# Down-projection weights in 16 KB runs, and a hidden activation turned in four shifted blocks

## The reference, cut to what matters

```
for e in range(32):
    y = (silu(t @ w_gate[e]) * (t @ w_up[e])) @ w_down[e]     # 1024 -> 512 -> 1024
    out = out + combine[:, e:e+1] * y
```

## Time and profile before

| | |
|---|---|
| median of three runs | 893.41 us (892.76 to 894.4) |
| time of the profiled execution | 893.44 us |
| its span, first to last instruction | 891.8 us |
| mean granted TensorE clock over the span | 0.980 |
| busy: PE, PEld, DVE, ACT, POOL | 92%, 64%, 37%, 23%, 17% |
| DMA packets in all | 71744, 265.18 MB |

### The profile page before, as it was taken

The page is one execution under the profiler, slowest core; times in us unless marked ns, Lnnn a source line. Parts: engine busy times, 40 slices in busy tenths (PEclk is TensorE's granted clock), DMA queues, the critical chain, the costliest instruction groups (busy, mean ns, idle before and its releaser), DMA issues.

```text
span 891.8 us, 15452 instructions
## 1 busy us (share of the span) xinstructions
PE 821.4 (92%) x5317; PEld 569.0 (64%) x5318; DVE 330.2 (37%) x616; ACT 200.7 (23%) x296; POOL 155.8 (17%) x241
## 2 busy tenths in 40 slices
PE   7999999999999999999899999989989999997860
PEld 6888887888888888886455554455545555544430
DVE  3799997841645246258111011110111101110107
ACT  4633435142643324141000000000000000000003
POOL 4232901000220000010212222112202222112100
PEclk9999999999999999999999999999999999999995
DMA  8693321723234938559999999999999999999977
GB/s 256 144 181 113 103 86 19 179 80 134 72 118 162 408 122 315 225 207 347 418 421 419 417 423 420 425 423 424 424 421 423 424 423 425 422 424 422 423 324 276
DMA packets 71744, 265.18 MB, mean 297 GB/s; under 512 B 29526, under 2 KB 30550, under 8 KB 54516
## 3 DMA queue, kind: packets, MB, share of 16 engines
q1 hardware_dynamic: 65428, 254.10, 74.8%
q0 software_dynamic: 6128, 10.45, 3.1%
q10 hardware_dynamic: 144, 0.02, 0.0%
HBM read 256.59 MB, written 16.52 MB: 306 GB/s over the span
## 4 chain that ended last, share of the span: by engine, by line
PE 78%; SPq 6%; DMA 6%; DVE 5%; issue 2%; ACT 2%; POOL 0%; DVEq 0%; POOLq 0%; ACTq 0%
PE ps L1095 36%; PE ps L465 22%; PE ps L481 11%; DMA slot_x<-in_exp_w_gate 5%; SPq L448 4%; PE ps L1080 2%; SPq L446 2%; PE ps L471 1%; DVE pair L716 1%; DVE pair L721 1%; PE ps L1072 1%; DVE hl L773 1%; PE ps L603 1%; DMA ssm<-choice_rows 1%; SPq L493 0%
## 5 line engine op out<-in xcount | busy, mean ns | idle before, releaser
L716 DVE TENSOR_TENSOR pair<-pair,ps 128x256 f32<-128x256 f32 x32 | 13.5, 421 | 334.9 <-PE ps L465 334.9
L1095 PE MATMUL ps<-h_hi,w_hi 128*128 128x512 f32 x280 | 109.2, 390 | 0.0
L1095 PE MATMUL ps<-h_hi,w_lo 128*128 128x512 f32 x280 | 109.0, 389 | 0.0
L1095 PE MATMUL ps<-h_lo,w_hi 128*128 128x512 f32 x280 | 108.9, 389 | 0.0
L1530 DVE TENSOR_TENSOR w_lo<-raw,w_hi 128x1024 fp32r<-128x1024 f32 x56 | 72.5, 1296 | 95.6 <-ACT w_hi L1334 94.9
L1334 ACT CAST w_hi<-raw 128x1024 fp32r<-128x1024 f32 x59 | 62.1, 1056 | 188.2 <-PE ps L1095 188.2
L465 PE MATMUL ps<-ssm,pair 128*64 128x256 f32 x832 | 95.2, 384 | 5.8 <-DMA ssm<-in_exp_w_gate 4.2
L465 PEld LDWEIGHTS ps<-ssm,pair 128*64 128x64 f32 x832 | 63.0, 139 | 42.5 <-issue 17.2
L787 ACT COPY late<-ps 128x512 f32<-128x512 f32 x35 | 20.5, 587 | 296.3 <-PE ps L481 296.3
L877 POOL DMA_INDIRECT choice_rows<-late,put_now x35 | 35.6, 1018 | 289.3 <-ACT late L787 239.9
L1095 PEld LDWEIGHTS ps<-h_hi,w_lo 128*128 128x128 f32 x280 | 52.6, 188 | 11.0
(11 more groups left out here) (342 smaller groups left out, 1225.4 us busy)
## 6 DMA issues: line engine op xcount, KB each, us to landing
ssm<-in_exp_w_gate SPq DMA_DIRECT2D x16, 2048.0 KB, 21.5
raw<-in_w_in SPq DMA_DIRECT2D x40, 512.0 KB, 3.9
au<-in_exp_w_up SPq DMA_DIRECT2D x8, 2048.0 KB, 24.8
ssm<-in_exp_w_up SPq DMA_DIRECT2D x8, 2048.0 KB, 21.0
ssm<-in_exp_w_down SPq DMA_DIRECT2D x8, 2048.0 KB, 21.4
hl<-in_exp_w_down SPq DMA_DIRECT2D x8, 2048.0 KB, 25.0
slot_x<-in_exp_w_gate SPq DMA_DIRECT2D x8, 2048.0 KB, 29.3
raw<-in_exp_w_down SPq DMA_DIRECT2D x8, 2048.0 KB, 28.0
```

Source lines behind the costliest of these rows:

```text
L716: nc.vector.tensor_tensor(act_cols, silu_cols, up_now, ALU.mult).then_inc(act_ready, 1)
L1095: t = nc.tensor.matmul(bank, lhs, rhs, start=k == 0 and n == 0, stop=k == 2 * count - 1 and n == 2)
```

## The change

Down weights are read as index (p, j): partition p holds the hidden rows 4p to 4p+3 in one run of 16 KB. So hidden half h now belongs to partitions 64h to 64h+63 of the down weights. In set 3 the two halves stay: j 0 and 1, then j 2 and 3, 8 KB each on a partition.

The product is written as 4 blocks of 64 columns (a step of four words on both operands), and a second instruction repeats the first block as a fifth. TensorE turns four blocks of 128 columns, each shifted by 64, so that block j holds hidden columns j of the lower half on partitions 0 to 63, and columns j+1 on partitions 64 to 127. VectorE copies the lower partitions of it (64 x 256), ScalarE the upper ones of the other half in two instructions (64 x 192 and 64 x 64). TensorE waits for both. Of `turn_x`, three transposes now stand ahead of `turn_act` and one behind. The down product has as many matmuls as before, of the same shapes.

```diff
-        silu, act_ = pair[:, 1024:1280], pair[:, 1280:1536]
-        actT = pair[:, 1536:1792].rearrange("p (j n) -> p j n", j=2)
+        silu, act_ = pair[:, 1024:1280], pair[:, 1536:1536 + (KF + 1) * CAP]
+        actT = pair[:, 1280:1536].rearrange("p (j n) -> p j n", j=KF)
...
-                 "down": exp_w_down[0].rearrange("e (h p j) n -> e p h (j n)", p=P, j=2)}
+                 "down": exp_w_down[0].rearrange("e (p j) n -> e p (j n)", p=P)}
...
-        at_bank = ps[:, B_AT, 0:256].rearrange("p (j n) -> p j n", j=2)
-        up_now, silu_cols = (a.rearrange("p (c j) -> p j c", j=2) for a in (ps[:, B_UP, 0:F // 2], silu))
-        act_cols = act_.rearrange("p (j c) -> p j c", j=2)
+        at_bank = ps[:, B_AT].rearrange("p (j n) -> p j n", j=KF)
+        up_now, silu_cols = (a.rearrange("p (c j) -> p j c", j=KF) for a in (ps[:, B_UP, 0:F // 2], silu))
+        act_cols = act_.rearrange("p (j c) -> p j c", j=KF + 1)
...
         def turn_act():
-            for j in range(2):
-                t = nc.tensor.transpose(at_bank[:, j], act_[:, P * j:P * (j + 1)], ident[:])
+            for j in range(KF):
+                t = nc.tensor.transpose(at_bank[:, j], act_[:, CAP * j:CAP * j + P], ident[:])
             return t
+        def low_half(copy):
+            return copy(actT[0:CAP], at_bank[0:CAP, :, 0:CAP])
+        def high_half(copy):
+            copy(actT[CAP:P, 1:KF], at_bank[CAP:P, 0:KF - 1, CAP:P])
+            return copy(actT[CAP:P, 0], at_bank[CAP:P, KF - 1, CAP:P])
...
-                    t = nc.tensor.matmul(ps[CAP * c:CAP * (c + 1), bank], actT[:, j, CAP * h:CAP * (h + 1)],
-                                         w[:, 2 * h + j, W * c:W * (c + 1)], start=n == 0, stop=n == 3)
+                    t = nc.tensor.matmul(ps[CAP * c:CAP * (c + 1), bank], actT[:, j], w[:, j, W * c:W * (c + 1)],
+                                         start=j == 0, stop=j == KF - 1)
+        def activated():
+            nc.vector.tensor_tensor(act_cols[:, 0:KF], silu_cols, up_now, ALU.mult)
+            return nc.vector.tensor_tensor(act_cols[:, KF], silu_cols[:, 0], up_now[:, 0], ALU.mult)
...
-                turn_x(pe, xg[after], 0, 2)
+                turn_x(pe, xg[after], 0, 3)
                 pe.wait_ge(act_ready, e + 1)
                 turn_act().then_inc(at_full, 1)
-                turn_x(pe, xg[after], 2, 4).then_inc(xt_full, 1)
-                pe.wait_ge(actT_ready, e + 1)
+                turn_x(pe, xg[after], 3, 4).then_inc(xt_full, 1)
+                pe.wait_ge(actT_ready, e * 2 + 2)
...
-            nc.vector.tensor_tensor(act_cols, silu_cols, up_now, ALU.mult).then_inc(act_ready, 1)
+            activated().then_inc(act_ready, 1)
...
-            nc.vector.tensor_copy(actT, at_bank).then_inc(actT_ready, 1)
+            low_half(nc.vector.tensor_copy).then_inc(actT_ready, 1)
...
             def turn(e, b, nth, first):
+                if not first:
+                    gated(e, False)
+                act.wait_ge(at_full, e + 1)
+                if not first:
+                    act.wait_ge(done["down"], e)
+                high_half(nc.scalar.copy).then_inc(actT_ready, 1)
```

More of the change, by code:

```diff
@@ L373, in trunk @@
         OV_XGT, OV_PRODUCT, OV_ACTT, OV_DVE = 1, 2, 3, 3
-        OV_SILU, OV_RES, OV_ACT = 1, 2, 2
+        OV_SILU, OV_ACTT_HIGH, OV_RES, OV_ACT = 1, 2, 3, 3
         def full(eng, name):
@@ L435, in weights @@
             dst = slots[EW[w][kind]]
[L436 to L440, removed]
+            if not isinstance(e, int):
                 src = src.rearrange("e p n -> (e p) n")
             if w == SETS - 1 and kind != "gate":
-                if kind == "up":
-                    dst, src = slot_runs[EW[w][kind]], src.rearrange("p (h n) -> p h n", h=2)
+                dst, src = slot_runs[EW[w][kind]], src.rearrange("p (h n) -> p h n", h=2)
                 for h, half_in in enumerate((signal, rest_in[kind])):
@@ L519, in experts_sync @@
             weights(sp, 3, "up", 3, ew_in[3]["up"])
-            down3, down3_src = slot_runs[EW[3]["down"]], w_src["down"][3]
+            down3, down3_src = slot_runs[EW[3]["down"]], w_src["down"][3].rearrange("p (h n) -> p h n", h=2)
             def residual_half(h, half_in):
@@ L637, in experts_tensor @@
             banks_free(6, 7)
-            pe.wait_ge(actT_ready, 1)
+            pe.wait_ge(actT_ready, 2)
             pe.wait_ge(ew_in[0]["down"], 16)
@@ L678, in second_block @@
                     turn_act().then_inc(at2_full, 1)
-                    pe.wait_ge(actT2_ready, before + 1)
+                    pe.wait_ge(actT2_ready, before * 2 + 2)
                     pe.wait_ge(res2_ready, before + 1)
@@ L703, in over @@
                 pe.wait_ge(ov_dve, o_ * OV_DVE + OV_ACTT)
-                if not first:
-                    pe.wait_ge(ov_act, o_ * OV_ACT)
+                pe.wait_ge(ov_act, o_ * OV_ACT + OV_ACTT_HIGH)
                 down(0, B_RES[0]).then_inc(ov_pe, 1)
@@ L736, in second_part @@
                     v.wait_ge(second_done, before * 3 + 3 + DONE["up"])
[L737 removed]
+                    activated().then_inc(act2_ready, 1)
                     v.wait_ge(at2_full, before + 1)
[L739 removed]
+                    low_half(nc.vector.tensor_copy).then_inc(actT2_ready, 1)
             second_part(0)
@@ L756, in over @@
                     v.wait_ge(done["down"], NE)
-                nc.vector.tensor_copy(actT, at_bank).then_inc(ov_dve, 1)
+                low_half(nc.vector.tensor_copy).then_inc(ov_dve, 1)
             each_over(v, over)
@@ L804, in turn @@
                     nc.scalar.activation(silu, ps[:, B_GATE, 0:HALF], ACT.Silu).then_inc(silu2_ready, 1)
+                    act.wait_ge(at2_full, before + 1)
+                    high_half(nc.scalar.copy).then_inc(actT2_ready, 1)
                     results(res2, B_RES2, second_done, before * 3 + 3 + DONE["down"], res2_ready, second_rows, before * 16 + 16)
@@ L830, in over @@
                 nc.scalar.activation(silu, ps[:, B_GATE, 0:HALF], ACT.Silu).then_inc(ov_act, 1)
+                act.wait_ge(ov_pe, o_ * OV_PE + OV_AT)
+                if first:
+                    act.wait_ge(done["down"], NE)
+                high_half(nc.scalar.copy).then_inc(ov_act, 1)
                 if first:
```

8 lines of the change are left out of this document (3 added, 5 removed).

## The result

The changed kernel takes 905.62 us (median of four runs, 902.73 to 907.0) where the kernel before takes 893.4. The ratio is 1.0132 (95% interval 1.0118 to 1.0146): slower by 1.3%, clear of the noise, 2.0 us from the predicted 903.6 and inside the range. The profiled execution took 904.46 us for a span of 902.7.

What follows compares the result with a forecast made beforehand. The DMA stream was taken to set the end, TensorE 13.8 us ahead; 34 passes of 0.69 us add 23.5, making TensorE last, with a span of 902.0 us and 903.6 predicted, range 894.5 to 912.

Steps and rivals of the forecast that it cites:

- TensorE becomes last: Expert stage: TensorE's chain, not the DMA stream, sets the end, reaching expert 31 at 860.6 us.
- The slack of 13.8 us: At expert 31's gate product: without weight waits TensorE would start at 837.1 us instead of 850.86; added work is free up to this.
- its weights have landed some ten microseconds before: Expert 31's gate weights land at 848.8 to 850.9 us, before TensorE's chain arrives at 860.6.
- The step of four words: VectorE's products of silu and up: SBUF operand pays 0.24 us a pass over 256 + 64 columns, bounds 0 and 0.47.
- both operands pay: Rival at VectorE's products: SBUF and PSUM operands both pay for the step, d 0.92, time 911.7 us; 14 in 100.
- The second product: VectorE's 128x64 product for the repeated block: 222 ns less 0.08 overlap adds 0.14 us a pass.
- Four transposes for two: TensorE's turning of the activation: 0.72 us for four against 0.44 for two adds 0.28 us a pass.
- The copies: After the transposes: VectorE's half stays 0.42 us, ScalarE's two pieces end 0.03 later; 0.03 us a pass, bounds 0 and 0.15.
- d: What one pass from up to down gets longer: 0.14 + 0.24 + 0.28 + 0.03 = 0.69 us.
- the formula: Whole kernel, as long as TensorE is last: time = 879.5 + 35 d, crossing the old time at d = 0.40.
- the 0.2 that I took off for the down weights: Behind expert 31's gate product: the wait for the second half of the down weights, 0.49 us idle, loses 0.2.
- what could break the sum: Named risks: TensorE fetching longer loop code (single gaps of 1 to 2 us), both operands slowing the product, transposes under a hidden gap.

Runs made afterwards that it cites:

- the doses: The kernel before with one, two or four extra VectorE 128x64 products between up and down in each pass: 892.77, 893.54 and 896.69 us.
- contiguous form: The changed kernel with both operands of the silu-and-up products read contiguously, output not the reference's: 896.88 us, ratio 1.0042.
- longer runs alone: The kernel before with only the down weights loaded in 16 KB runs, output not the reference's: 891.45 us, ratio 0.9979.
- one operand: The changed kernel with ScalarE writing silu in block order, so only the PSUM operand keeps the step of four words: 897.29 us, ratio 1.0052.
- Early: The changed kernel with silu in block order and the main product announced alone; only the fourth transpose waits for the repeated block: 895.47 us, ratio 1.0025.
- pieces: The changed kernel with silu in block order and the product in three separately announced pieces, two token-row transposes on either side: 895.68 us, ratio 1.0019.
- Four products: The kernel before with four extra VectorE 128x64 products behind each silu-and-up product, ahead of the signal to TensorE: 896.69 us, ratio 1.0045.
- the two empty ones: The kernel before with a never-run branch of 28 or 4 transposes in TensorE's loop, most likely left out at build: 893.55 and 892.95 us.

## Why the prediction was right, and where it was lucky

**TensorE becomes last: shown.** The chain of after is on TensorE through the whole expert stage with no weight load, its waits for DMA there are gone, and the doses show slack first and the price behind it (0.26 x 34 costs nothing, 0.52 x 34 does). The slack of 13.8 us at the very end carried the case. Its other half, "its weights have landed some ten microseconds before", did not hold: they landed at 813.41 + 40.1 = 853.5, 6.6 us before the product and later than the 848.8 to 850.9 of the prediction, which took the DMA stream as independent of TensorE. Here that changed nothing; in two forms below it did.

**The step of four words: shown, size right.** Taken as 0.24 us a pass, it measured 0.24 (contiguous form against after). The groups by form of the kernel after, 425 to 900 us, against the earlier trace rows:

```profile
L488 DVE TENSOR_TENSOR pair<-pair,ps 128x256 f32<-128x256 f32 x34 | 20.9, 615 | 344.0 <-PE ps L460 344.0
...
L489 DVE TENSOR_TENSOR pair<-pair,ps 128x64 f32<-128x64 f32 x34 | 8.6, 253 | 0.0
```

615 against 421 ns is 0.76 ns a column, where the eight-word reduction had given 0.73. That not both operands pay was right too: with the step on the PSUM operand alone the product took 421 ns. For the SBUF operand the Trainium skill, "SBUF — State Buffer", section "Door 1: The DMA port swizzle", wants at least two hits in a line of 16 bytes for full rate. The traces agree: a step of two words is free (421 ns), one of four isn't (615 ns).

**The second product: right.** 0.14 with the step's part in the other term; one more product of 128x64 put the period at 12.22, 0.12 more.

**Four transposes for two: over-sized.** I took the row of four in a row, 0.72, minus 0.44. In the place itself they take 0.66, so 0.23 instead of 0.28: the row came from another stage.

**The copies: over-sized.** 0.48 from the copies to the down product before and after, so nothing instead of 0.03. ScalarE's pieces are 0.31 and 0.21, as worked out, and the half on VectorE sets the same 0.42. Their small errors together with the 0.02 at the product make d 0.59 and not 0.69.

**What hid that.** With the measured d the formula gives 879.5 + 35 x 0.59 = 900.2, 4.3 us below the profiled execution. The sum lacked 3.0 us ahead of expert 31 (837.1 + 34 x 0.59 = 857.2, found 860.15) and 1.3 behind it (902.7 - 860.15 = 42.55 us, where I had 40.9 - 0.2 + 0.59 = 41.3). The two errors, +3.5 us from 35 x 0.10 and -4.3, nearly cancel in this execution; against the median the formula is 5.4 short. That the forecast came within 2.0 us is luck in this part. Behind expert 31, 1.1 us is the scatter of its rows, 3.54 us in the chain of after and 2.41 in that of before, and the 0.2 that I took off for the down weights wasn't there: from the start of the last down product to the copy of its result it is 3.70 us in both kernels. Of the 3.0 us ahead of it, 2.9 can be placed. TensorE's waits of 425 to 870 us that nothing releases, in the kernel before and in the one after (sum, count, longest):

```profile
PE ps L465 <- issue: 4.4, 3, 2.1
```
```profile
PE ps L460 <- issue: 5.6, 4, 1.9
```

That is 1.2 us more, in one more wait of the kind that the prediction had named as what could break the sum: it stands in the loop's first pass, at 498.69 in the chain, and 31 instruction packets were loaded instead of 30. Another 1.7 us is the clock of one execution, just ahead of the stage. The same windows of the kernel before and of the one after (us, busy time of PE, PEld, DVE, ACT and POOL with instructions, granted clock, DMA share, GB/s):

```profile
407.00:409.00 2.00, 2.00 (x12) 0.70 (x10) 1.90 (x13) 0.00 (x0) 0.00 (x0) 1.00 1.00 297
```
```profile
405.00:407.00 2.00, 2.00 (x12) 0.97 (x11) 1.89 (x10) 0.00 (x0) 0.00 (x0) 0.72 1.06 354
407.00:409.00 2.00, 2.00 (x6) 0.49 (x4) 1.90 (x14) 0.00 (x0) 0.00 (x0) 0.50 0.97 295
409.00:411.00 2.00, 2.00 (x12) 0.79 (x10) 1.71 (x8) 0.00 (x0) 0.00 (x0) 0.92 1.02 430
```

TensorE ran at 0.50, the 1.2 GHz level, for part of these six microseconds: (0.28 + 0.50 + 0.08) x 2 = 1.7 us. Sixteen matmuls of L609 took 5.35 us there; before (L603), and with the longer runs alone, the same ones took 3.65. TensorE had been idle for 1.74 us just before, but with the longer runs alone too, where the clock stayed at 1.00.

**The cost of the four-block form besides d, and what of it stays open.** Set d into the forecast and compare the medians. After: 900.2 by the formula, 905.6 measured, 5.4 more. Contiguous and one operand, both d = 0.35: 879.5 + 12.25 = 891.8, 5.1 and 5.5 more. Early and pieces, where DMA is last: 891.45 with the longer runs alone plus d in the last expert, 891.7 and 891.6, 3.8 and 4.1 more. Four products on the kernel before: 1.0 less. So everything built on the four-block form carries about 4 to 5 us that no step of mine holds, and its executions spread wider: 4.3 us in after (4 runs), 6.4 with one operand (4), 5.6 early (12), 6.0 in pieces (12), though only 2.6 in the contiguous one (4). Those built on the kernel before spread 1.4 to 2.8 (4 to 11 runs), TensorE last (four products, 1.4) or not, and the kernel before itself 3.5 in 27.

In the profiled executions nearly all of it has a place.

*Gaps in the first pass.* The five profiles of the form have four gaps in the first pass instead of the three of all seven profiles without it (the kernel before, longer runs alone, the doses, the two empty ones); they sum to 5.6 to 7.6 us, against 3.0 to 4.4. Longer code is a candidate, but it is one instruction packet more, and the two runs meant to test it were the empty ones.

*The DMA stream runs short once.* SyncE may issue a load only when TensorE is through with that buffer, so early in the stage the stream hangs on TensorE. The gate weights of expert 15 are issued at 585.13 before, 10.4 us ahead of the landing of the load before them (595.5); with the longer runs alone at 584.57. With early blocks they are issued at 590.81, only 4.2 us ahead of that landing (573.27 + 21.7 = 595.0), and in pieces at 593.25, 2.6 ahead (575.75 + 20.1 = 595.85):

```profile
590.81 0.33 SPq L443 DMA_DIRECT2D slot_x<-in_exp_w_gate  x1
```

The same window of the longer runs alone, early blocks and pieces (columns as above; the last one is GB/s):

```profile
588.00:600.00 12.00, 11.20 (x84) 6.13 (x84) 0.75 (x3) 0.97 (x2) 2.42 (x4) 1.00 1.00 421
```
```profile
588.00:600.00 12.00, 10.83 (x84) 5.83 (x82) 0.97 (x3) 1.20 (x4) 0.18 (x1) 1.00 0.93 373
```
```profile
588.00:600.00 12.00, 10.05 (x80) 5.90 (x81) 1.66 (x4) 1.30 (x4) 1.21 (x2) 1.00 0.81 318
```

At 421 GB/s the missing bytes are 1.4 and 2.9 us of transfer, and expert 31's gate product starts at 849.75 and 851.71, 0.7 and 2.7 us later than with the longer runs alone (849.01). The 6.2 us by which early blocks are late at 590.81 come from 12 passes of 0.22 (2.6 us) and from the gaps of the first pass, 6.5 against 3.2. The other forms have the dip too: 358 contiguous, 347 with one operand, 296 in after. The kernel with four products issues the same load at 590.38 and keeps 415, so being late is not enough; that it takes the longer runs as well is likely and was not isolated.

*Behind expert 31.* The scatter of its rows takes 2.41 us in the chain of before, 3.54 in after, 4.04 contiguous, 2.57 with one operand, and 3.04 with the longer runs alone, so it varies without the form too. With early blocks and in pieces it is 2.41, but the last read of `choice_rows` takes 7.4 to 7.5 instead of 6.2.

These terms give the profiled executions back. Contiguous (895.69, 3.9 above the formula): 2.0 of gaps, 1.6 of scatter and the 0.2. One operand (894.00, 2.2 above): 1.6, 0.2 and 0.2. Early and pieces (893.86 and 895.85) against the profiled execution of the longer runs alone (892.25), 1.6 and 3.6 more: 0.7 and 2.7 at the gate, 0.2 of d, 0.6 behind expert 31. Four products (896.59, 1.1 below): 1.4 less of gaps, and the 0.2.

Three things stay open: why the form has a fourth gap and longer ones; whether the dip needs the form or only its lateness and the longer runs; and what the other executions hold, since the profiled ones of contiguous, one operand and early are 1.2, 3.3 and 1.6 us below their medians. A wider spread would follow if gaps that vary pass through the dip to the end, but no trace of a slower execution shows it.

**No better version came out of it.** The longer runs save 1.8 us. The cheapest complete ways of using them here (early, 895.47, and in pieces, 895.68) are 10 us better than the change and 2 us worse than before.

## What to carry to other kernels

When two resources look full, find the one that the chain ends with and the slack of the other at the very end; an edit on the other is free up to that slack in all, and beyond it is paid once for every pass, so 0.1 us in d is 3.4 us here. Ask as well what feeds the full one: here the loads wait for TensorE's buffers, so a TensorE that is 6 us late at 590 us already moved the landings that its slack was counted against. A DMA gain of 1.8 us can't carry a TensorE loss of 20. Where the engine writing a buffer has time, let it do the reordering (silu in block order cost ScalarE nothing and saved 7 to 8 us), so that the engine on the path reads contiguously.

## What was not expected of the hardware

- VectorE takes 615 ns for 256 columns with a step of four words on the SBUF and the PSUM operand, and 421 in each of three others: both contiguous, that step on the PSUM operand alone, a step of two words on both.
- Runs of 16 KB instead of 8 KB gave 0.09 us a load of 2 MB, ratio 0.9979.
- Turning eight 64x64 blocks in 16 small matmul records took 0.68 us, no longer than four full transposes (0.66), but the kernel lost 84 us, with 87 instruction packets instead of 30 and 21 gaps of up to 6.3 us between 425 and 870 us.
